# Norms over heads: block-of-ones products in place of pick and spread

## The reference

```
q, k   = rope(rmsnorm(heads of 64)), sparse attention
kk     = kk / max(sqrt(sum over a head of 64 of kk*kk), 1e-12)     (RWKV-7)
q, km  = rmsnorm(heads of 128)                                     (memory)
h      = x + (sum of sigmoid gates * up-projections) @ w_out
out    = h + expert layer (8 heads, 16 experts for each token)
rmsnorm(t) = t * rsqrt(mean(t*t) + 1e-6) * gain
```

## Time and profile before

| | |
|---|---|
| median of 3 runs | 1093.55 us (1093.04 to 1094.9) |
| the profiled execution | 1094.59 us |
| its span, first to last instruction | 1092.8 us |
| PE busy | 862.2 us (79%) |
| DVE busy | 651.5 us (60%) |
| ACT busy | 396.5 us (36%) |
| POOL busy | 324.8 us (30%) |
| gathers of experts, share of 16 DMA engines | 58.3% |
| mean granted clock of PE | 0.868 |

### The profile page before, as it was taken

How to read it: one execution, slowest core, us unless ns; L and a number is a source line. 1 busy time by engine, 2 the same in 40 slices (tenths; PEclk the granted TensorE clock), 3 DMA queues, 4 the chain that set the end, 5 groups by cost and what they waited for, 6 DMA issues and landing times.

```text
span 1092.8 us, 16392 instructions
## 1 busy us (share of the span) xinstructions
PE 862.2 (79%) x5770; PEld 523.1 (48%) x5770; DVE 651.5 (60%) x1563; ACT 396.5 (36%) x1105; POOL 324.8 (30%) x294
## 2 busy tenths in 40 slices
PE   9999999999999999877677677667657556566565
PEld 8888888878888878643233233213111111111111
DVE  3453532186544243778768757767766866876774
ACT  2025133213412011453454444534434434434443
POOL 0000000020003000444444443454444455455441
PEclk9999999999999999987897897888676776767857
DMA  8443333222212267699999999999999999999996
GB/s 319 148 154 115 117 116 106 88 78 94 94 46 79 79 236 288 272 397 427 427 426 425 428 427 426 426 427 427 425 426 426 428 427 428 428 428 427 427 428 283
DMA packets 46586, 329.82 MB, mean 302 GB/s; under 512 B 5312, under 2 KB 5568, under 8 KB 6976
## 3 DMA queue, kind: packets, MB, share of 16 engines
q0 software_dynamic: 36864, 268.45, 58.3%
q1 hardware_dynamic: 9104, 58.86, 14.6%
q10 hardware_dynamic: 560, 1.70, 0.4%
HBM read 327.95 MB, written 1.05 MB: 301 GB/s over the span
## 4 chain that ended last, share of the span: by engine, by line
PE 47%; DMA 27%; DVE 14%; ACT 5%; issue 5%; POOL 0%; POOLq 0%; DVEq 0%; ACTq 0%
DMA pool_mem<-in_experts,pool_mem 27%; PE psum_proj L630 18%; DVE pool_mem L1896 6%; PE psum_job L1038 6%; PE psum_proj L1013 4%; PE psum_proj L979 3%; PE psum_job L859 3%; PE psum_proj L643 3%; DVE pool_mem L1790 1%; PE psum_proj L997 1%; PE psum_job L997 1%; ACT pool_mem L1343 1%; DVE pool_mem L1787 1%; ACT pool_mem L1340 1%; DVE pool_mem L1840 1%
## 5 line engine op out<-in xcount | busy, mean ns | idle before, releaser
L1038 PE MATMUL psum_job<-pool_mem 64*64 64x512 f32 x2048 | 351.9, 799 | 208.3 <-ACT pool_mem L1343 208.0
L1965 POOL DMA_INDIRECT pool_mem<-in_experts,pool_mem x256 | 302.7, 1182 | 413.4 <-PE psum_job L1038 271.6
L1896 DVE CUSTOM_DVE_ANT_0 pool_mem<-pool_mem 128x1024 f32<-128x1024 f32 x256 | 309.8, 1224 | 166.9 <-DMA pool_mem<-in_experts,pool_mem 165.8
L1038 PEld LDWEIGHTS psum_job<-pool_mem 64*64 64x64 f32 x2048 | 84.2, 163 | 457.1 <-issue 455.9
L630 PE MATMUL psum_proj<-pool_mem 128*128 128x256 f32 x896 | 197.3, 380 | 0.7 <-ACT pool_mem L1142 0.7
L630 PEld LDWEIGHTS psum_proj<-pool_mem 128*128 128x128 f32 x896 | 169.3, 190 | 25.5 <-issue 2.7
L1336 ACT ACTIVATE pool_mem<-pool_mem 128x1 f32<-128x1 f32 x256 | 51.5, 201 | 265.9 <-DVE pool_mem L1896 263.8
L1953 POOL TENSOR_TENSOR pool_mem<-pool_mem,const 128x256 f32<-128x256 f32 x24 | 16.6, 713 | 332.9 <-DVE pool_mem L1643 273.0
L1343 ACT ACTIVATE pool_mem<-const,pool_mem 128x64 f32<-128x64 f32 x256 | 89.1, 348 | 18.4
L1340 ACT ACTIVATE pool_mem<-pool_mem 128x1 f32<-128x1 f32 x256 | 75.4, 294 | 9.3
L1013 PE MATMUL psum_proj<-pool_mem 128*128 128x256 f32 (+1 forms) x320 | 66.2, 364 | 3.7 <-ACT pool_mem L1366 2.5
(11 more groups left out here) (270 smaller groups left out, 810.6 us busy)
## 6 DMA issues: line engine op xcount, KB each, us to landing
pool_mem<-in_weights SPq DMA_DIRECT2D x51, 1024.0 KB, 4.8
pool_mem<-in_experts,pool_mem POOLq DMA_INDIRECT x256, 12.3
pool_mem<-in_xT SPq DMA_DIRECT2D x1, 1024.0 KB, 4.8
pool_mem<-in_memT SPq DMA_DIRECT2D x1, 1024.0 KB, 10.4
pool_mem<-in_x ACTq DMA_DIRECT2D x1, 1024.0 KB, 12.3
const<-in_const SPq DMA_DIRECT2D x1, 985.5 KB, 14.3
rows<-in_rows SPq DMA_DIRECT2D x1, 512.0 KB, 16.4
pool_mem<-in_ffn_gain ACTq DMA_DIRECT2D x1, 512.0 KB, 16.0
```

Of the source, the lines that this page charges most:

```text
L1038: ins = mm(sum_bank(t, d)[sum_strip(i, d), :], lhsT=diag[rows_, g % DIAGS, :], rhs=slot[g % SLOTS][rows_, D + 512 * d:D + 512 * d + 512], ...
L1896: ins = V.tensor_tensor_reduce(u, u, xn_tok[:, t, :], 1.0, 0.0, ALU.mult, ALU.add, hid[:, par, s_:s_ + 1])
L1965: G_.indirect_dma_start(slot[s_ % SLOTS], None, t_in["experts"], bass.IndirectOffsetOnAxis(ap=expert_i[:, par, s_:s_ + 1], axis=0)).then_i ...
```

## The change

The sums are made by products with a matrix of ones (heads of 128 channels) or one with two blocks of 64x64 ones (heads of 64, the new constant pair_ones), one product for each chunk. Each channel so has its head's sum at once, in two banks for each norm. ACT takes two roots of 512 columns each, DVE one reciprocal of 1024 columns, in place where the squares stood, and multiplies from SBUF in one instruction of 1024 columns. The second products (spread) and their jobs are gone. PE waits for new semaphores scaled_ok before the memory scores and before each rope, where it waited for the reads of the spread banks. The constants lose 736 columns of 128 rows; the tile small grows from 208 to 304 columns and is not used further. SCHEDULE is not changed: its "spread" steps are now DVE's alone.

```diff
-for _name, _n in [("ident", 128), ("headsel", 2), ("pick_pairs", 128), ("pick_ones", 224), ("rot", 128), ("causal", 128),
-                  ("gram_mask", 4 * CHUNK), ("level", CHUNK * LEVELS), ("iota", 16), ("inv_freq", 1), ("two_idents", CHUNK), ("to_heads", W)]:
+for _name, _n in [("ident", 128), ("headsel", 2), ("pair_ones", 128), ("rot", 128), ("causal", 128),
+                  ("gram_mask", 4 * CHUNK), ("level", CHUNK * LEVELS), ("iota", 16), ("inv_freq", 1), ("two_idents", CHUNK)]:
...
+    out["pair_ones"] = p[:, None] // HD == p[None, :] // HD
...
+def square_jobs(x):
+    return [(x + "_ss", i) for i in range(2)]
...
-        small = sb("small", [P, 208])
+        small = sb("small", [P, 304])
...
+        stat = {"kn": part(Q0 + 32 * K1, CT, S), "mk": mem_sq["mk"], "mq": mem_sq["mq"], "q": rope_sq["q"], "k": rope_sq["k"]}
...
+        scaled_ok = {x: sem("scaled_ok_" + x) for x in ("mk", "mq", "q", "k")}
...
-            def spread(x):
-
-                n = SUMS[x]
-                w = n // CT
-                pe.wait_ge(rms_ok[x], 1)
-                for i, job in enumerate(spread_jobs(x)):
+                whole = ones if SUMS[x] == CT else c("pair_ones")
+                for i, job in enumerate(square_jobs(x)):
                     o = halves(begin(job))
                     for m in range(2):
-                        k = 2 * i + m
-                        to_chunk = ident[:, 32 * k:32 * k + 1].to_broadcast([P, P]) if w == 1 else \
-                            c("to_heads")[:, k * P:(k + 1) * P]
-                        ins = mm(o[:, m, :], lhsT=to_chunk, rhs=stat[x], start=True, stop=True)
+                        ins = mm(o[:, m, :], lhsT=whole[:, :], rhs=sq[:, 2 * i + m, :], start=True, stop=True)
                     end(ins, job)
...
-            spread("kn")
...
-            spread("mk")
-            spread("mq")
...
-            for job in spread_jobs("mk") + spread_jobs("mq"):
-                wait_read(pe, job)
+            for x in ("mk", "mq"):
+                pe.wait_ge(scaled_ok[x], 1)
...
             def rope(x):
-                for job in spread_jobs(x):
-                    wait_read(pe, job)
+                pe.wait_ge(scaled_ok[x], 1)
...
+                for i, job in enumerate(square_jobs(x)):
+                    wait_job(act, job)
+                    job_read(A(stat[x][:, 2 * i:2 * i + 2, :], halves(bank(job)), ACT.Sqrt, scale=1.0 / n, bias=eps_col), job)
...
             def inverse_roots(x):
                 V.reciprocal(stat[x], stat[x]).then_inc(rms_ok[x], 1)
+                dve.wait_ge(rms_ok[x], 1)
...
-            wait_job(dve, ("kn_ss",))
-            job_read(V.tensor_scalar(stat["kn"], bank(("kn_ss",))[:, 0:S], 1e-24, None, ALU.max),
-                     ("kn_ss",))
+            for i, job in enumerate(square_jobs("kn")):
+                wait_job(dve, job)
+                job_read(V.tensor_scalar(stat["kn"][:, 2 * i:2 * i + 2, :], halves(bank(job)), 1e-24, None, ALU.max), job)
...
-            for i, job in enumerate(spread_jobs("kn")):
-                wait_job(dve, job)
-                job_read(V.tensor_tensor(kk[:, 2 * i:2 * i + 2, :], kk[:, 2 * i:2 * i + 2, :], halves(bank(job)),
-                                         ALU.mult), job)
-            for job in spread_jobs("kn"):
-                wait_read(dve, job)
+            st(V.tensor_tensor(kk, kk, stat["kn"], ALU.mult)).wait()
...
-            for x, dst in (("mk", kmT), ("mq", mqT)):
-                for i, job in enumerate(spread_jobs(x)):
-                    wait_job(dve, job)
-                    job_read(V.scalar_tensor_tensor(dst[:, 2 * i:2 * i + 2, :], dst[:, 2 * i:2 * i + 2, :],
-                                                    v(x + "_gain"), halves(bank(job)), ALU.mult, ALU.mult), job)
+                V.scalar_tensor_tensor(dst, dst, v(x + "_gain"), stat[x], ALU.mult, ALU.mult).then_inc(scaled_ok[x], 1)
...
             def scaled(x):
-                for i, job in enumerate(spread_jobs(x)):
-                    wait_job(dve, job)
-                    job_read(V.scalar_tensor_tensor(rope_sq[x][:, 2 * i:2 * i + 2, :], rope_raw[x][:, 2 * i:2 * i + 2, :],
-                                                    v(x + "_gain"), halves(bank(job)), ALU.mult, ALU.mult), job)
-                for job in spread_jobs(x):
-                    wait_read(dve, job)
+                V.scalar_tensor_tensor(rope_sq[x], rope_raw[x], v(x + "_gain"), stat[x], ALU.mult, ALU.mult).then_inc(scaled_ok[x], 1)
+                dve.wait_ge(scaled_ok[x], 1)
                 st(V.tensor_tensor(qk_dst[x], rope_sq[x], trig[:, 0:1, :].to_broadcast([P, CT, S]), ALU.mult))
```

More of the change, by code:

```diff
@@ L157, in stage_jobs @@
     if kind == "sumsq":
-        return [(a[0] + "_ss",)]
-    if kind == "spread":
-        return spread_jobs(a[0])
+        return square_jobs(a[0])
     if kind == "rope":
@@ L653, in square_sums @@
             def square_sums(x, sq):
[L655 to L657 removed]
+                if SUMS[x] == 1:
+                    o = begin((x + "_ss",))[:, 0:S]
                     for k in range(KT):
                         ins = mm(o, lhsT=ones[:, :], rhs=sq[:, k, :], start=(k == 0), stop=(k == KT - 1))
[L660 to L673 removed]
+                    end(ins, (x + "_ss",))
+                    return
+                whole = ones if SUMS[x] == CT else c("pair_ones")
+                for i, job in enumerate(square_jobs(x)):
                     o = halves(begin(job))
                     for m in range(2):
[L676 to L679 removed]
+                        ins = mm(o[:, m, :], lhsT=whole[:, :], rhs=sq[:, 2 * i + m, :], start=True, stop=True)
                     end(ins, job)
@@ L981, in up @@
                 ins.then_inc(proj_full, 1)
-            stages = {"sumsq": sumsq, "spread": spread, "rope": rope, "gram": gram_matrices, "inverse": inverse, "rhs": chunk_rhs,
+            stages = {"sumsq": sumsq, "rope": rope, "gram": gram_matrices, "inverse": inverse, "rhs": chunk_rhs,
                       "u": chunk_u, "y": chunk_y, "out": chunk_out, "score": attention_scores,
@@ L1111, in root @@
             def root(x, n):
-                wait_job(act, (x + "_ss",))
-                dst = {"x": x_rn, "mem": mem_rn}[x] if SUMS[x] == 1 else stat[x]
-                job_read(A(dst, bank((x + "_ss",))[:, 0:S], ACT.Sqrt, scale=1.0 / n, bias=eps_col),
-                         (x + "_ss",))
+                if SUMS[x] == 1:
+                    wait_job(act, (x + "_ss",))
+                    dst = {"x": x_rn, "mem": mem_rn}[x]
+                    job_read(A(dst, bank((x + "_ss",))[:, 0:S], ACT.Sqrt, scale=1.0 / n, bias=eps_col),
+                             (x + "_ss",))
+                    return
+                for i, job in enumerate(square_jobs(x)):
+                    wait_job(act, job)
+                    job_read(A(stat[x][:, 2 * i:2 * i + 2, :], halves(bank(job)), ACT.Sqrt, scale=1.0 / n, bias=eps_col), job)
             squares("x", nT)
@@ L1147, in _ @@
             A(p_ex, p_ex, ACT.Exp, scale=-DECAY).then_inc(sg["decay_ok"], 1)
-            wait_read(act, ("kn_ss",))
+            for job in square_jobs("kn"):
+                wait_read(act, job)
             A(stat["kn"], stat["kn"], ACT.Sqrt).then_inc(sg["kroot"], 1)
@@ L1497, in _ @@
             for x, dst in (("mk", kmT), ("mq", mqT)):
-                wait_read(dve, (x + "_ss",))
+                for job in square_jobs(x):
+                    wait_read(dve, job)
                 inverse_roots(x)
-            for x, dst in (("mk", kmT), ("mq", mqT)):
-                for i, job in enumerate(spread_jobs(x)):
-                    wait_job(dve, job)
-                    job_read(V.scalar_tensor_tensor(dst[:, 2 * i:2 * i + 2, :], dst[:, 2 * i:2 * i + 2, :],
-                                                    v(x + "_gain"), halves(bank(job)), ALU.mult, ALU.mult), job)
+                V.scalar_tensor_tensor(dst, dst, v(x + "_gain"), stat[x], ALU.mult, ALU.mult).then_inc(scaled_ok[x], 1)
             dve.wait_ge(sg["trig_ok"], 1)
```

23 lines of the change are left out of this document (4 added, 19 removed).

## The result

The changed kernel takes a median of 1101.09 us (1098.58 to 1102.12, 5 runs), the kernel before beside it 1094.54 us (1093.04 to 1095.31, 5 runs). The ratio is 1.0058 with an interval of 1.0047 to 1.0069: slower by 6.4 us. The forecast was slower by 4.1 us, a ratio of 1.0037. The profiled execution took 1101.09 us with a span of 1099.3 us, so 6.5 us more than the profiled execution before, and that is the sum that can be taken apart.

The account below looks back on a forecast made before the run. PE's order of work bounds the first half, moving the end one for one; expert gathers fill DMA in the second. -3.8 (first place) + 5.4 (second) + 2.5 (clock) = +4.1 us: 1097.6 us, range 1094.8 to 1101.0.

Parts of the forecast that it names:

- The long operation: DVE's five norm reciprocals, widened from 256 to 1024 columns, take 6.55 us each instead of 1.75, 24 us more in all.
- First place: Norms of kn, mk, mq: long reciprocals of mk and mq are hidden, PE gains 0.35 + 3.46 = 3.8 us.
- lower bound of 3.3: Lower end of the gain at kn, mk, mq, 3.3 us instead of 3.8, if ACT's delays add up.
- Second place: Norms of q and k: PE waits 9.8 us for scaled q; rope k starts 5.4 us later.
- The clock: After PE's wait ahead of rope q the clock is low for 5 us, 2.5 us lost, ends 0 and 3.4.
- POOL beside DVE: POOL's masks run while DVE scales q, which can cost DVE some tenths.
- Rival 2's far end: Reciprocals ahead of rope q no longer than now: PE would not wait, about -8 us, 1085.5; whole rival 0.06.
- last step: Rope k's delay, 1.6 us plus the clock's part, is kept up to the last instruction.
- Constants: 736 columns (377 KB) less to load, hidden behind the projections of mem_k and mem_v; counted as nothing.

Follow-up runs that it names:

- e2: Changed kernel with the reciprocals of mk and mq taken on the first 256 columns only; 1100.58 us, ratio 1.006.
- a_again: The changed kernel run once more, unaltered, for a second trace and more times; 1100.79 us, ratio 1.0058.
- b: Kernel before the change with the unused tile small at 304 columns instead of 208, nothing else; 1102.57 us, ratio 1.0084.
- e9: e7 with the squares of mq moved behind the projection idx_q; 1089.8 us, ratio 0.996.
- e5: Changed kernel with the tile small at 208 columns instead of 304; 1108.28 us, ratio 1.0119.
- e3: Changed kernel with PE's wait ahead of the rotation of q filled by 42 products of ones; 1096.5 us, ratio 1.0024.
- e1: Changed kernel with the reciprocals of q and k taken on the first 256 columns only; 1096.94 us, ratio 1.0017.
- e4: Changed kernel with the change undone for q and k (old constants back), small still at 304 columns; 1101.8 us, ratio 1.0068.
- e8: e4 with small at 208 columns, so all tiles stand where they stood before the change; 1092.52 us, ratio 0.9983.
- e7: Changed kernel with ACT's logarithm and exponential in place of DVE's reciprocals for q and k; 1089.03 us, ratio 0.9953.
- e6: Changed kernel with one gate unit moved from behind the first y to ahead of the spread of q; 1092.27 us, ratio 0.9981.

## Why the prediction was right, and where it was off

The direction, the place and the mechanism were as forecast, and the size was too small. 1101.09 us lies 3.5 us above the forecast and just above the upper end of its range, but the kernel before was 1 us slower beside it than the forecast had it. By the ratio, on the forecast's own 1093.55 us, it is 1099.9 us: inside the range and 2.3 us above the forecast, and the forecast's ratio of 1.0037 lies below the measured interval. The steps:

- **The long operation.** 6.55 us was forecast from two sizes on one line, 6.55 us is in every row (one has 6.54), 32.8 us for five. By the repeat count in the Trainium skill, "VectorE: DVE Perf Modes", section on the fixed hardware budget, it was an estimated 8.7 us, and the trace doesn't agree: the rows of 256 and 1024 columns give (6.55 - 1.75) / 768 = 6.25 ns a column, three quarters of that estimate's 8.3.
- **First place.** The reciprocals of mk and mq are hidden, as e2 shows. Both gains came: from the start of mem_q to the memory scores it takes 56.74 us before (97.98 to 154.72) and 53.02 after, 3.72 us less, against 3.8, and a_again against b gives 3.71. The offset at the scores is 3.34 all the same, because mem_q itself starts 0.38 us late. 0.17 of this is there already at the squares of mk, ahead of any norm's work, and 0.21 comes between these and mem_q, where ACT takes two roots for mk; 0.15 was forecast for them and carried in the rounding. So the lower bound of 3.3 ("ACT's delays add up") was the better number. In front of the squares of mq PE now stands for 1.22 us, which the row calls issue. ACT's read of mem_q was forecast to be late next, and that is the cause that fits: in e9, where mem_q was read long before, nothing stands in front of them. e9 puts a price on that wait: 1.5 us for PE once other work stands ahead.
- **Second place.** A wait of 9.8 us was forecast, 10.0 us is measured. Without the spreads (4.10 us) and the short stop before (0.29) that is 5.6 us net, against 5.4.
- **The clock.** 2.5 us were forecast from a guess of 5 us at the lower level. Measured: 5.3 us and 2.5 us in the changed kernel's first profile, 1.9 us in a_again, 2.3 us in e5, 1.5 us in e2 (3.51 us for the rotation, 1.15 for the inverse, after the same wait of 10.00). e3 gives it back. That the first profile hit the guess is luck; the four together say 1.5 to 2.5.
- **POOL beside DVE** was named as costing some tenths: the second product (L1551) takes 1.54 us and the next 1.66, with 1.23 forecast. They lie behind the scaling of q; PE's rotation of k, which needs the second, starts 2.4 us after it has ended.
- **Rival 2's far end fell**: if the reciprocals were no longer than now, PE would not wait, I wrote, and the kernel would be at 1085.5. e1 has such reciprocals, PE waits 5.2 us and the kernel is at 1096.94. The order on DVE (reciprocal of k and masks ahead of the scaling of q) is a wait of its own, which the spreads used to cover. Nor does each microsecond less in one shorten the wait by two, as I wrote: 4.8 us less in each shortened it by 4.8. My own list of times had DVE waiting for the roots of k, and the rival was priced without it.
- **What failed is the last step, that from the gate unit on everything is carried through unchanged.** The offset grew by 1.3 us up to the output projection and by 0.45 in the expert layer. Of the 1.3 us, 0.97 arise over the stop in front of the last 122 of 256 small products and 0.36 over that at 328 us. In a_again the first is 0.69 (0.46 shown as idle). It is in every profile of a kernel whose PE stream has the changed length, with 0.46 to 0.82 us shown, and in e4 and e8 too, with 1.10 and 0.83, after 118 of the products and not 134; it is absent in the two kernels with the old stream (before and b) and in e3, whose 42 products more shift all that follows. So it seems to go with the place in the instruction stream, not with the norms. What makes PE stop there wasn't tried and stays open. The stop at 328 us goes with q and k: it is in the seven profiles where DVE takes their reciprocals in the new form, e1 and e3 among them, and in none of the six others (before, b, e4, e7, e8, e9). Why it arises there stays open too. As to the expert layer, from the transposes to the end it takes 634.9 us in the two kernels whose tiles all stand where they stood (before, e8) and 635.3 to 636.0 in the eight whose tiles stand 2560 bytes lower. With one profile each that may be chance or the place once more.
- **Constants** were counted at nothing, and the load was. But the sentence missed that their size moves the slots of the gathers. The change got away with it, since the 96 unused columns of small keep the address modulo 512 bytes. With small left at 208 the change would have cost 13 us (e5), twice as much.

By its parts the change is, at the memory scores, a gain of 3.3 us, then a net wait of 5.6, a clock loss of 1.5 to 2.5 and 1.0 to 1.3 us of stops.

## What to carry to other kernels

An operation whose time grows with its columns should run on the narrow form, unless another engine waits for nothing while it runs: here the same long reciprocal was free for mk and mq and cost PE 4.8 us of waiting for q and k, and what the clock took on top. Ask in which order the waiting engine has its work, for a unit moved forward (e6) or the operation given to an idle engine (e7) turned a loss of 6.4 us into gains of 2 and 5. When a tile or a constant changes its size, keep the address of the buffers of a DMA-bound stage, and read the GB/s of that stage afterwards.

## What the runs showed of the hardware that was not expected

- An unused tile that is 384 bytes wider costs 0.8% of the kernel: gathers into slots 128 or 384 bytes off move 421 GB/s and not 427.
- The clock fell to 0.50 around waits of PE of 2.9 (e6), 5.2 (e1) and 10.0 us, and cost 1.6, 2.3 and 1.5 to 2.5 us: in these profiles the price hardly depends on the length of the wait. After 2.21 us (e7, e9) it didn't fall. Near 400 us, with the same gaps of 1.56 or 1.57 and 0.72 us in front, it fell in eight of the thirteen profiles and not in the other five (15.5 to 15.7 or 14.05 us for the same 64 instructions). That is 1.5 to 1.7 us of difference between executions of equal work, so two single profiles are compared only with this in view.
- The dense work starts at one of two times, whatever the kernel: the projection of mem_q at 98.0 to 98.5 us in nine profiles and at 99.7 to 100.1 in four (b, a_again, e3, e6). The changed kernel has both, 98.36 and 100.01. At 464 us 0.6 of these 1.65 us are left; the rest is what clock and stops cost less in a_again (0.6 and 0.2 us at the two falls of the clock, 0.3 at the stop).
- A stream of small products can stop for 0.46 to 1.10 us with nothing to wait for, at a place that shifts with the stream's length.
